# Block three of a fused float32 kernel: the convolution's norms, tile by tile, among the rounds of the output projection

## The reference, cut to what matters

```python
def conformer_conv(u, gate, conv_w, conv_b, ln_g, ln_b):
    ...
    y = y + conv_b
    y = layer_norm_3(y, ln_g, ln_b)
    return jax.nn.silu(y)

def third_block(x, ...):
    ...
        c = conformer_conv(u, gate, conv_w[l], conv_b[l], conv_ln_g[l], conv_ln_b[l])
        mix = jnp.concatenate([rms_norm_3(a, attn_out_g[l]), rms_norm_3(c, conv_out_g[l])], axis=-1)
        x = x + mix @ w_out[l]
        h = rms_norm_3(x, norm_mlp_g[l])
        x = x + jnp.square(jax.nn.relu(h @ w_mlp_up[l])) @ w_mlp_down[l]
    return x
```

## Time and profile before

| what | value |
|---|---|
| time, median of 3 runs | 3556.02 us (3552.03, 3556.02, 3556.64) |
| time of the profiled execution | 3551.65 us |
| its span (first to last instruction) | 3549.8 us |
| PE, PEld, DVE busy | 89%, 68%, 58% of the span |
| ACT, POOL busy | 34%, 12% |
| mean granted TensorE clock | 0.945 of full speed |
| from `window_over` to the first product of the projection | 33.4 us (2683.5 to 2716.9) |
| the projection's eight products with what lies between them | 115.2 us (2716.9 to 2832.1) |
| from there to the MLP's first product | 15.3 us (2832.1 to 2847.4) |

### The profile page before, as it was taken

The page is one execution under the profiler, slowest core; times in us unless marked ns, Lnnn a source line. Parts: engine busy times, 40 slices in busy tenths (PEclk is TensorE's granted clock), DMA queues, the critical chain, the costliest instruction groups (busy, mean ns, idle before and its releaser), DMA issues. The chain is left out here.

```text
span 3549.8 us, 37585 instructions
## 1 busy us (share of the span) xinstructions
PE 3158.0 (89%) x14208; PEld 2405.1 (68%) x14208; DVE 2058.2 (58%) x3113; ACT 1198.8 (34%) x2280; POOL 435.5 (12%) x407
## 2 busy tenths in 40 slices
PE   6999999886788879899997786989876999999999
...
DMA packets 189934, 326.63 MB, mean 92 GB/s; under 512 B 16242, under 2 KB 110610, under 8 KB 189754
## 3 DMA queue, kind: packets, MB, share of 16 engines
...
...
## 5 line engine op out<-in xcount | busy, mean ns | idle before, releaser
L215 PE MATMUL banks<-b3h4a_hi,b3mlpw_part 128*128 128x512 f32 x1024 | 318.8, 390 | 6.8 <-DVE b3mlpw_part L3281 6.8
L215 PE MATMUL banks<-b3mlpw_part,b3mlp_acthi 128*128 128x512 f32 x1024 | 315.2, 389 | 0.0
L215 PE MATMUL banks<-b1ln_w,b_hThi 128*128 128x512 f32 x768 | 239.5, 393 | 0.0
L215 PEld LDWEIGHTS banks<-b3h4a_hi,b3mlpw_part 128*128 128x128 f32 x1024 | 192.9, 188 | 47.3 <-issue 7.1
L3328 DVE TENSOR_TENSOR b3out_x<-b3out_x,banks 128x1024 f32<-128x1024 f32 x128 | 154.6, 1218 | 111.7 <-PE banks L215 111.7
L215 PEld LDWEIGHTS banks<-b3mlpw_part,b3mlp_acthi 128*128 128x128 f32 x1024 | 192.2, 188 | 39.9
L3298 ACT ACTIVATE b3mlp_relu<-banks 128x1024 f32<-128x1024 f32 x32 | 32.9, 1029 | 497.9 <-PE banks L215 497.9
L215 PE MATMUL banks<-b3out_lo,b3mlpw_part 128*128 128x512 f32 x512 | 199.6, 390 | 0.0
L215 PE MATMUL banks<-b3mlpw_part,b3mlp_actlo 128*128 128x512 f32 x512 | 199.2, 389 | 0.0
L508 PE MATMUL banks<-b_hThi,b1item_hi 128*128 128x512 f32 x464 | 195.4, 421 | 3.4 <-DVE b1item_lo L497 3.1
L508 PE MATMUL banks<-b_hThi,b1item_lo 128*128 128x512 f32 x464 | 183.5, 396 | 0.0
...
## 6 DMA issues: line engine op xcount, KB each, us to landing
...
```

The costliest lines, as they stand in the source:

```text
L215: last = pe.matmul(out, x, y, start=i == 0, stop=i == n - 1)
```

## The change

One stage per engine, `*_out3`, takes the place of two. The norms run tile by tile: `normed` (the two DVE instructions of the first norm), `squares` (sum of squares and the 1e-6, now per tile), `finished` (`z`). Three tiles of `normed`, two of `squares` and one of `finished` stand ahead of the loop; in round r DVE does `normed(r+3)`, `squares(r+2)`, `finished(r+1)` and then the round's own work, in which the addition now stands first and `lo` last. PE turns tile r+1 of `z` at the start of round r, ahead of the product of tile r. The turned `h` has one pair of banks instead of two. All the roots of the stretch are powers on GpSimd, which also takes over the reciprocals. `y` lies in `K.slot[0]`, `z` has 3 buffers instead of 8, and the MLP's first two weight items are sent after the last `z`. The `x3` tiles are sent ahead of the projection instead of at its start.

```diff
--- before.py
+++ after.py
@@ -2773,8 +2773,6 @@
     L.start(sp, "w_out3_0", K.slot[1], columns(K.dr["w_out_3"][0], 0, 512))
     sp.wait_ge(S["q3_mm"], ST)
     L.start(sp, "w_out3_1", K.slot[2], columns(K.dr["w_out_3"][0], 512, 512))
-    for n in range(2):
-        L.start(sp, ("mlp", n), item_tiles(K.m5.stage[n], n), item_source(K, n))
 def pe_gate(K):
@@ -3060,143 +3058,176 @@
-def sp_norm3(K):
-    sp, L, m = K.sp, K.loads, K.m3n
+def sp_out3(K):
+    sp, S, L, n, m = K.sp, K.S, K.loads, K.m3n, K.m4
     window_over(K, sp)
-    for tile, name in ((m.gl, "conv_ln_g_3"), (m.bl, "conv_ln_b_3"), (m.gout, "conv_out_g_3")):
+    for tile, name in ((n.gl, "conv_ln_g_3"), (n.bl, "conv_ln_b_3"), (n.gout, "conv_out_g_3")):
         L.start(sp, name, tile, rows(K.dr[name][0]))
...
+    for st in range(ST):
+        L.start(sp, ("x3", st), m.x3[:, st], K.x3_dram[st * P:(st + 1) * P, :])
+    sp.wait_ge(*S.at("n3_turned", ST))
+    L.start(sp, "gm", m.gm, rows(K.dr["norm_mlp_g_3"][0]))
+    sp.wait_ge(*S.at("n3_z", ST))
+    for i in range(2):
+        L.start(sp, ("mlp", i), item_tiles(K.m5.stage[i], i), item_source(K, i))
+def pe_out3(K):
+    pe, S, n, m = K.pe, K.S, K.m3n, K.m4
     window_over(K, pe)
     for st in range(ST):
         transposed(pe, K.bank[st], [K.m3.acc[i][:, st * P:(st + 1) * P] for i in range(4)], K.eye).then_inc(S["n3_turned"], 1)
-    for st in range(ST):
-        pe.wait_ge(*S.at("n3_copied", st + 1))
+    def turned(st):
+        if st < 2:
+            pe.wait_ge(*S.at("n3_copied", ST))
+        else:
+            pe.wait_ge(*S.at("n3_mix", st - 1))
         pe.wait_ge(*S.at("n3_z", st + 1))
-        transposed(pe, K.bank[st], [m.z[:, st, k * P:(k + 1) * P] for k in range(HV)], K.eye).then_inc(S["n3_turned"], 1)
...
+        transposed(pe, K.bank[6 + st % 2], [n.z[st % 3][:, k * P:(k + 1) * P] for k in range(HV)], K.eye).then_inc(S["n3_turned"], 1)
+    turned(0)
+    for half in range(2):
+        pe.wait_ge(*K.loads[f"w_out3_{half}"])
+    for r in range(ST + 2):
+        if r + 1 < ST:
+            turned(r + 1)
+        if r < ST:
+            if r >= 2:
+                pe.wait_ge(*S.at("o3_x", r - 1))
+            pe.wait_ge(*S.at("n3_mix", r + 1))
+            for half in range(2):
+                last = natural(pe, K.pair[r % 2][:, half * 512:(half + 1) * 512], K.m3.mixT, r, K.slot[1 + half], 0, 512)
+            last.then_inc(S["o3_mm"], 1)
+        st = r - 2
+        if st >= 0:
+            if st:
+                pe.wait_ge(*S.at("o3_lo", st))
+            pe.wait_ge(*S.at("o3_h", st + 1))
+            transposed(pe, K.pair[2], [m.h[st % 2][:, k * P:(k + 1) * P] for k in range(KT)], K.eye).then_inc(S["o3_turned"], 1)
+def act_out3(K):
+    a, S, n, m = K.a, K.S, K.m3n, K.m4
     window_over(K, a)
     for st in range(ST):
         a.wait_ge(*S.at("n3_turned", st + 1))
-        a.activation(m.y[:, st], K.bank[st], ACT.Copy).then_inc(S["n3_copied"], 1)
...
+        a.activation(n.y[:, st], K.bank[st], ACT.Copy).then_inc(S["n3_copied"], 1)
+    def silu(st):
+        a.wait_ge(*S.at("n3_y", st + 1))
+        a.activation(n.y[:, st], n.y[:, st], ACT.Silu).then_inc(S["n3_silu"], 1)
+    def mixed(st):
+        a.wait_ge(*S.at("n3_turned", ST + st + 1))
+        a.activation(K.m3.mixT[:, HV:KT, st * P:(st + 1) * P], by_k(K.bank[6 + st % 2]), ACT.Copy).then_inc(S["n3_mix"], 1)
+    for st in range(3):
+        silu(st)
+    mixed(0)
+    for r in range(ST + 2):
+        if r + 3 < ST:
+            silu(r + 3)
+        if r + 1 < ST:
+            mixed(r + 1)
+        st = r - 2
+        if st >= 0:
+            a.wait_ge(*S.at("o3_turned", st + 1))
+            a.activation(m.hi[:, :, st * P:(st + 1) * P], by_k(K.pair[2]), ACT.Copy).then_inc(S["o3_hi"], 1)
+def pool_out3(K):
+    g, S, n = K.g, K.S, K.m3n
+    def power(x):
+        return g.tensor_tensor(x, x, K.half.to_broadcast([P, x.shape[1]]), ALU.pow)
+    g.wait_ge(*S.at("n3_ms", 1))
+    power(n.rs[:, 0]).then_inc(S["n3_root"], 1)
+    for i in range(3, ST + 4):
+        if i == 3:
+            for st in range(3):
+                g.wait_ge(*S.at("n3_ms", 2 + st))
+                power(n.rs[:, 1, st:st + 1]).then_inc(S["n3_root"], 1)
+        if i < ST:
+            g.wait_ge(*S.at("n3_ms", 2 + i))
+            power(n.rs[:, 1, i:i + 1]).then_inc(S["n3_root"], 1)
+        st = i - 3
+        if st < ST:
+            g.wait_ge(*S.at("o3_ms", st + 1))
+            power(K.stat[st][:, 1:2]).then_inc(S["o3_root"], 1)
+def dve_out3(K):
+    v, S, vs, n, m = K.v, K.S, K.vs, K.m3n, K.m4
+    window_over(K, v)
     def then(instruction):
         vs.mark(instruction)
         v.wait_ge(vs.sem, vs.n)
-    window_over(K, v)
+    def normed(st):
+        if st >= ST:
+            return
+        then(v.scalar_tensor_tensor(n.y[:, st], n.y[:, st], n.mv[:, st, 0:1], n.gl, ALU.subtract, ALU.mult))
+        v.scalar_tensor_tensor(n.y[:, st], n.y[:, st], n.rs[:, 0, st:st + 1], n.bl, ALU.mult, ALU.add).then_inc(S["n3_y"], 1)
+    def squares(st):
+        if st >= ST:
+            return
+        if st >= 3:
+            v.wait_ge(*S.at("n3_turned", ST + st - 2))
+        v.wait_ge(*S.at("n3_silu", st + 1))
+        then(v.tensor_tensor_reduce(n.z[st % 3], n.y[:, st], n.y[:, st], 1.0 / W2, 0.0, ALU.mult, ALU.add, n.rs[:, 1, st:st + 1]))
+        v.tensor_scalar(n.rs[:, 1, st:st + 1], n.rs[:, 1, st:st + 1], RMS3_EPS, None, ALU.add).then_inc(S["n3_ms"], 1)
+    def finished(st):
+        if st >= ST:
+            return
+        v.wait_ge(*S.at("n3_root", 2 + st))
+        v.scalar_tensor_tensor(n.z[st % 3], n.y[:, st], n.rs[:, 1, st:st + 1], n.gout, ALU.mult, ALU.mult).then_inc(S["n3_z"], 1)
     for st in range(ST):
         v.wait_ge(*S.at("n3_copied", st + 1))
-        then(v.bn_stats(m.stats[:, st], m.y[:, st]))
-        vs.mark(v.bn_aggr(m.mv[:, st], m.stats[:, st]))
+        then(v.bn_stats(n.stats[:, st], n.y[:, st]))
+        vs.mark(v.bn_aggr(n.mv[:, st], n.stats[:, st]))
     v.wait_ge(vs.sem, vs.n)
-    v.tensor_scalar(m.rs[:, 0], m.mv[:, :, 1], RMS3_EPS, None, ALU.add).then_inc(S["n3_ms"], 1)
+    v.tensor_scalar(n.rs[:, 0], n.mv[:, :, 1], RMS3_EPS, None, ALU.add).then_inc(S["n3_ms"], 1)
     for name in ("conv_ln_g_3", "conv_ln_b_3", "conv_out_g_3"):
         v.wait_ge(*K.loads[name])
     v.wait_ge(*S.at("n3_root", 1))
-    then(v.reciprocal(m.rs[:, 0], m.rs[:, 0]))
...
+    normed(0)
+    normed(1)
+    squares(0)
+    normed(2)
+    squares(1)
+    finished(0)
     for r in range(ST + 2):
-        st = r - 2
...
+        normed(r + 3)
+        squares(r + 2)
+        finished(r + 1)
         if r < ST:
-            if r >= 2:
...
+            v.wait_ge(*K.loads[("x3", r)])
+            v.wait_ge(*S.at("o3_mm", r + 1))
+            v.tensor_tensor(m.x3[:, r], m.x3[:, r], K.pair[r % 2], ALU.add).then_inc(S["o3_x"], 1)
         st = r - 1
         if 0 <= st < ST:
-            a.wait_ge(*S.at("o3_ms", st + 1))
...
+            h, s = m.h[st % 2], K.stat[st]
             if st == 0:
                 v.wait_ge(*K.loads["gm"])
             if st >= 2:
                 v.wait_ge(*S.at("o3_turned", st - 1))
             v.wait_ge(*S.at("o3_x", st + 1))
-            square_stats(K, v, K.stat[st], h, m.x3[:, st], RMS3_EPS).then_inc(S["o3_ms"], 1)
+            square_stats(K, v, s, h, m.x3[:, st], RMS3_EPS).then_inc(S["o3_ms"], 1)
             v.wait_ge(*S.at("o3_root", st + 1))
-            square_scale(K, v, K.stat[st], h, m.x3[:, st], m.gm).then_inc(S["o3_h"], 1)
...
+            v.scalar_tensor_tensor(h, m.x3[:, st], s[:, 1:2], m.gm, ALU.mult, ALU.mult).then_inc(S["o3_h"], 1)
+        st = r - 2
+        if st >= 0:
+            v.wait_ge(*S.at("o3_hi", st + 1))
+            cols = slice(st * P, (st + 1) * P)
+            v.tensor_tensor(m.lo[:, :, cols], by_k(K.pair[2]), m.hi[:, :, cols], ALU.subtract).then_inc(S["o3_lo"], 1)
@@ -3538,17 +3569,17 @@
     m.hot, m.tab = a.take("hot", [32, WIN_LEN]), a.take("tab", [32, NH])
     K.win_dram = [nc.dram_tensor(f"win{h}", (P, WIN_LEN), F32).ap() for h in range(NH)]
-    a, n = Space(nc, "b3norm", keep.at, TOP), Part()
...
     o = K.m4 = Part()
     o.hi = Space(nc, "b3h4a", K.area0, K.area1).take("hi", [P, KT, S_LEN], F32R)
     b, a = Space(nc, "b3outw", K.area1 + HT_BYTES, keep.at), Space(nc, "b3out", keep.at, TOP)
     o.x3, o.lo = a.take("x3", [P, ST, D]), a.take("lo", [P, KT, S_LEN], F32R)
     o.gm, o.h = b.take("gm", [P, D]), b.several("h", 2, [P, D])
+    n, more = Part(), Space(nc, "b3norm", a.at, TOP)
+    K.m3n = n
+    n.y = Space(nc, "b3normy", K.slots0, K.slots0 + SLOT_BYTES).take("y", [P, ST, W2])
+    n.gl, n.bl, n.gout, n.z = more.take("gl", [P, W2]), more.take("bl", [P, W2]), more.take("gc", [P, W2]), more.several("z", 3, [P, W2])
+    n.stats, n.mv, n.rs = more.take("stats", [P, ST, 6]), more.take("mv", [P, ST, 2]), more.take("rs", [P, 2, ST])
     w, b = K.m5, Space(nc, "b3mlp0", K.area1, keep.at)
```

(19 more changed lines are left out.)

2 lines of the change are left out of this document (removed).

## The result

The changed kernel takes 3604.02 us (median of 4 runs, 3599.17 to 3607.40) against 3555.96 us before (4 runs, 3552.03 to 3556.64): ratio 1.0139, 95% interval 1.0127 to 1.0150. It is **slower**, as forecast; 3601 was predicted, in a range of 3588 to 3612.

What follows compares the result with a forecast made beforehand. DVE's chain bounds the norms, PE the projection; the order of both streams makes them alternate. -11.9 + 47.9 + 7.0 + 4.3 = 47.3 us gives 3599.0 or 3603.4 by base; 3601 taken between, range 3588 to 3612.

Steps and rivals of the forecast that it cites:

- ahead of the first product: Norms before the projection: only the first tiles' norm steps remain there, so the first product starts 11.9 us earlier.
- gaps (without the products' own time): Between the projection's eight products: PE waits for DVE's addition, h, lo and norm steps; 53.1 us against 5.2, 47.9 more.
- slower products after idling: Projection products 0 to 6: each follows idle PE time and starts at a lower clock, 1.0 us each, 7.0 more.
- the end: Last product's end to the last lo's end: h(6) and lo(5) now come behind the last addition, 4.3 us more.
- outside the stretch: Code before the convolution's turns and from the MLP's first product on: no change, 0 us.
- The alternation: Projection rounds 1 to 6: PE and DVE wait for each other by turns instead of running side by side; 80%.
- The clock term: Projection products 0 to 6: PE's clock falls after idling, 1.0 us a product, 7.0 in all; ends 0 and 1.5 each.
- rival 3's powers: GpSimd powers inside h, five gaps and twice at the end: 1.52 us in place of 0.55, 6.8 us more.
- rival 3: Projection and end: GpSimd powers and two-input DVE instructions lock each other out, 11 us more, 3610 us; 8%.
- Two of the signs named: Projection: PE idle before z turns 4 us once, 7 to 9 five times; DVE waiting some 13 us for each product.
- Rival 1: Projection: the norms hide beside the products because PE need not wait for finished(r+1); -4.0 us, 3547.6; 5% with a variant.
- Rival 2: Projection gaps: PE's clock stays up, so the 7.0 us goes and z turns take 0.44; 3588.6 us; 7%.

Runs made afterwards that it cites:

- Experiments 1: The changed kernel with PE's turn of z(r+1) moved behind product r instead of ahead of it: 3549.13 us, ratio 0.9991 to the kernel before.
- experiment 4: The changed kernel with DVE's norm steps (normed, squares, finished) one round earlier, PE's order untouched: 3547.53 us, ratio 0.9984 to the kernel before.
- experiment 2: The changed kernel with each tile's last norm instruction on DVE (finished) done twice: 3607.09 us, ratio 1.0156 to the kernel before.
- 3: The changed kernel with the z turn behind the product and each tile's finished instruction on DVE done twice: 3550.87 us, ratio 0.9995 to the kernel before.
- Experiment 5: The changed kernel with turns of the identity matrix keeping PE busy while it waits for z of tiles 2 to 7: 3588.82 us, ratio 1.0101.
- experiment 6: The changed kernel with the roots of h back as square root on ScalarE and reciprocal on DVE: 3600.94 us, ratio 1.0129.
- Experiment 8: DVE's norms a round earlier and products halved, plus h(r-1) ahead of the addition, turned earlier, two bank pairs, h(7) before lo(6): 3531.65 us, ratio 0.9935.

## Why the prediction was right

| step of the sum | predicted | profile after |
|---|---|---|
| ahead of the first product | -11.9 | -12.2 |
| gaps (without the products' own time) | +47.9 | +45.3 |
| slower products after idling | +7.0 | +11.9 |
| the end | +4.3 | +3.8 |
| outside the stretch | 0 | +2.6 |
| sum | +47.3 | +51.3 |

- **The alternation**, the step that decided, holds as written: six gaps of 5.3, 8.7, 9.8, 9.8, 8.4 and 7.6 us (predicted 5.6, 9.2, 10.3, 10.3, 8.9, 8.0) and 0.87 in round 7. Experiments 1 and 4 remove it from either side, 2 and 3 price it. It could be read from the two engines' streams; the busy sums spoke for the opposite.
- The gaps were 2.6 too long in sum. The addition is followed by the sum of squares after 1.14, not 1.36: the wait for its own result costs nothing there. The power in `h` takes 0.67 with its handovers, not 0.76. And the z turn holds up the product for 0.88, not 1.0.
- **The clock term was mis-sized**: 1.0 a product was taken, 1.7 was paid (seven products, 109.2 recorded against 7 x 13.90). It differs between products of one profile (1.3 to 2.6) and between profiles (10.4 in experiment 2's, 13.6 in experiment 6's). I had taken one fall as 1.5 in all from the MLP's start, of which 0.5 went to the z turn. The upper end, 1.5 each, was too low as well. Experiment 5 shows that it is the idling: with PE kept busy, all six products that it covers take 13.90.
- The two errors, -2.6 and +4.9, partly cancelled; the 3601 owes its closeness in part to that, to the base taken between 3599.0 and 3603.4, and to the medians, which lie 48.1 apart where the two profiled executions lie 51.2 apart. The range's upper end is misadded: 3603.4 with rival 3's powers (6.8) is 3610, with all of rival 3 (11.2) 3615; 3612 is 3601 with all of it.
- Two of the signs named were right in kind and off in size. PE's idle time ahead of the z turns between products is 4.4 once, then 7.7, 7.9, 7.9, 6.5 and 5.7, where 7 to 9 five times was said. DVE waits 16.3 to 17.6 for each of the first seven products, not some 13: the wait also holds the z turn, the slower product and the handovers.
- **Start**: predicted 21.5 from the turns' start, measured 21.2. The eight-column power took 1.69 (1.67), DVE went on 1.90 after waiting began.
- **The end** is 4.3 against 3.8, by the same chain: `lo(5)`, then the turns of `h(6)` (2884.10), `lo(6)`, `h(7)` (2888.51). Experiment 8 undoes it.

```profile
2878.14 1.04 PE L206 MATMUL banks<-fixed_eye,b3outw_h 128*128 128x128 f32 x8
...
2882.83 1.22 DVE L3230 TENSOR_TENSOR b3out_lo<-banks,b3h4a_hi 128x1024 fp32r<-128x1024 f32 x1
...
2884.10 1.97 PE L206 MATMUL banks<-fixed_eye,b3outw_h 128*128 128x128 f32 x8 [4.92 <-DVE b3out_lo L3230]
...
2887.24 1.22 DVE L3230 TENSOR_TENSOR b3out_lo<-banks,b3h4a_hi 128x1024 fp32r<-128x1024 f32 x1
...
2888.51 1.97 PE L206 MATMUL banks<-fixed_eye,b3outw_h 128*128 128x128 f32 x8 [2.45 <-DVE b3out_lo L3230]
...
2891.57 1.23 DVE L3230 TENSOR_TENSOR b3out_lo<-banks,b3h4a_hi 128x1024 fp32r<-128x1024 f32 x1 [3.12 <-ACT b3h4a_hi L3137]
```

- *Rival 1* (the norms hide) fell, and its condition was named rightly: in experiment 4 `finished` stands a round earlier, and the time is 0.9984 of before, where it gave 3547.6 (0.9989); its sum had the sixth turn of `h` too. *Rival 2* fell: the clock was 0.87 over the products. *Rival 3* fell: `h`'s powers took 0.55; those beside a two-input DVE instruction took 0.99, until 0.41 after its end, as in the earlier trace rows, and nobody waited. DVE was not held up by them either: L3190 took 0.74 with a power beside it, the two-input instruction behind it 0.75 (they start at 2701.16 and 2701.82; the power runs from 2701.33 to 2702.33).
- Transfers: none was awaited in the stretch. The move of `x3` and of the MLP's items cost nothing, as said.
